# A two-block network on one core: the first block's mixers with all weight remainders on VectorE, and masked scores ahead of the short convolution

## The reference

```
h = rmsnorm(x, g_mix);  z = h @ w_in        # cut into a_b a_c a_h g_u g_v q k v q_idx k_idx w_idx d_a d_g
y_a = a_b * causal_dwconv3(a_c * a_h)
y_b = g_u * (tril(w_s) @ layernorm(g_v) + b_s)          # per chunk of 128 tokens and head
y_c = attention(rope(q), rope(k), v) over the 64 keys with the best index score
y_d = silu(layernorm(causal_dwconv31(d_a * sigmoid(d_g)) + b))
x = x + concat(y_a, y_b, y_c, y_d) @ w_out
x = x + (silu(rmsnorm(x) @ w_gate) * (rmsnorm(x) @ w_up)) @ w_down
```

## Time and profile before

| | us |
|---|---|
| median of 3 runs | 1291.46 (1290.04 to 1295.35) |
| the profiled execution | 1293.9, span 1292.1 |
| TensorE matmuls busy | 1145.1 (89%) |
| VectorE busy | 972.3 (75%) |
| ScalarE busy | 658.9 (51%) |
| GpSimd busy | 195.7 (15%) |

### The profile page before, as it was taken

How to read it: one execution, slowest core, us unless ns; L and a number is a source line. 1 busy time by engine, 2 the same in 40 slices (tenths; PEclk the granted TensorE clock), 3 DMA queues, 4 the chain that set the end, 5 groups by cost and what they waited for, 6 DMA issues and landing times.

```text
span 1292.1 us, 17395 instructions
## 1 busy us (share of the span) xinstructions
PE 1145.1 (89%) x6560; PEld 992.5 (77%) x6560; DVE 972.3 (75%) x1516; ACT 658.9 (51%) x935; POOL 195.7 (15%) x169
## 2 busy tenths in 40 slices
PE   3878779999997686799999899996499999999996
PEld 3757579999986485699999895674488888888885
DVE  5699669888546997588986544365888898889887
ACT  5323443333343233444443344534388888978885
POOL 4544100000034533000000100173300000000000
PEclk9879789999988796899999899997599999999998
DMA  9313136665742213467765511104157778787873
GB/s 381 134 65 129 67 130 230 242 246 225 278 181 82 104 45 151 186 270 319 306 262 220 206 66 66 65 1 179 82 227 294 301 285 315 276 318 275 320 274 139
DMA packets 23523, 256.52 MB, mean 199 GB/s; under 512 B 3120, under 2 KB 3248, under 8 KB 4912
## 3 DMA queue, kind: packets, MB, share of 16 engines
q1 hardware_dynamic: 23472, 255.86, 51.0%
HBM read 254.80 MB, written 1.05 MB: 198 GB/s over the span
## 4 chain that ended last, share of the span: by engine, by line
PE 75%; DVE 18%; issue 3%; ACT 2%; DMA 1%; POOL 1%; SPq 0%; DVEq 0%; POOLq 0%; ACTq 0%
PE bank L638 21%; PE bank L640 20%; PE bank L639 20%; DVE scratch L1676 5%; PE bank L629 3%; PE bank L1127 3%; PE bank L1110 3%; DVE w_l L1634 1%; DVE h_l L1640 1%; PE bank L898 1%; DMA m<-in_w_in 1%; DVE scratch L1775 1%; DVE w_l L2068 1%; DVE scratch L1730 1%; PE bank L973 1%
## 5 line engine op out<-in xcount | busy, mean ns | idle before, releaser
L2068 DVE TENSOR_TENSOR w_l<-m,w_h 128x1024 fp32r<-128x1024 f32 x196 | 239.2, 1254 | 19.8 <-ACT w_h L1499 19.5
L640 PE MATMUL bank<-h_h,fw_l 128*128 128x256 f32 x800 | 224.4, 281 | 0.0
L638 PE MATMUL bank<-h_h,fw_h 128*128 128x256 f32 x704 | 199.6, 284 | 8.3 <-issue 8.3
L1499 ACT ACTIVATE w_h<-m 128x1024 fp32r<-128x1024 f32 x200 | 198.0, 1050 | 14.0 <-DMA m<-in_experts 13.9
L639 PE MATMUL bank<-h_l,fw_h 128*128 128x256 f32 x704 | 197.8, 281 | 0.0
L1835 DVE TENSOR_TENSOR fw_l<-blocks_w,fw_h 128x1024 fp32r<-128x1024 f32 x132 | 156.3, 1220 | 2.9 <-ACT fw_h L1336 2.5
L640 PEld LDWEIGHTS bank<-h_h,fw_l 128*128 128x128 f32 x800 | 152.1, 190 | 0.0
L638 PEld LDWEIGHTS bank<-h_h,fw_h 128*128 128x128 f32 x704 | 133.5, 190 | 10.4 <-issue 8.7
L639 PEld LDWEIGHTS bank<-h_l,fw_h 128*128 128x128 f32 x704 | 134.0, 190 | 1.8
L1336 ACT ACTIVATE fw_h<-blocks_w 128x1024 fp32r<-128x1024 f32 x132 | 129.7, 1050 | 3.8 <-DMA blocks_w<-in_ffn 3.8
L1356 ACT ACTIVATE acts<-bank 128x256 f32<-128x256 f32 x44 | 16.9, 385 | 220.4 <-PE bank L640 220.4
(11 more groups left out here) (367 smaller groups left out, 2679.4 us busy)
## 6 DMA issues: line engine op xcount, KB each, us to landing
m<-in_experts SPq DMA_DIRECT2D x50, 2048.0 KB, 7.4
blocks_w<-in_ffn SPq DMA_DIRECT2D x22, 2048.0 KB, 7.6
m<-in_w_ada SPq DMA_DIRECT2D x24, 1024.0 KB, 8.4
m<-in_w_in SPq DMA_DIRECT2D x11, 2048.0 KB, 13.7
blocks_w<-in_ffn SPq DMA_DIRECT2D x22, 1024.0 KB, 4.9
m<-in_w_out SPq DMA_DIRECT2D x6, 2048.0 KB, 7.3
blocks_w<-in_w_in SPq DMA_DIRECT2D x2, 2048.0 KB, 21.3
m<-in_b_ada SPq DMA_DIRECT2D x2, 2048.0 KB, 7.7
```

The source lines that it names most:

```text
L638: pe.matmul(out_, xh, wh, start=first and i == 0, stop=False, skip_group_check=True)
L640: ins = pe.matmul(out_, xl, wh, start=False, stop=last and i == n - 1, skip_group_check=True)
L1499: act.activation(w_h[:, c % 3, at], m[:, c % 4, at], ACT.Copy).then_inc(hi_ready, 1)
L2068: dve.tensor_tensor(w_l[:, c % 4, at], m[:, c % 4, at], f32(w_h[:, c % 3, at]), ALU.subtract).then_inc(lo_ready, 1)
```

## The change

- All 30 remainders of a layer, and the rotation of q and k (`rotate_qk`), are on VectorE. GpSimd keeps norms, masks and the scaling of g_v.
- The rounded weights have other places: dadg in slot 3 of `m`, vqi in scratch, qk, ah and abac in `blocks_w`. So guv is loaded into slot 3 only when da and dg are done; abac and ah are loaded earlier; dg is computed before da, ah before ac and ab. `acc` of layer 0 is slot 1, so layer 1's qk is loaded behind the modulation sums.
- Layer 1's dadg and vqi are rounded and split during layer 0's FFN (blocks 7 to 9 and the last); its dadg is loaded after the first two pieces of `w_ada`.
- Of the 32 modulation sums 12 stay at the end of the FFN; 4 come before each of the two `tx1` transposes and 12 behind them. The sums are in bank 5 instead of 6.
- The four remainders of the first half of w_out are in rounds 4 to 7 of the top-k loop, those of the second half behind the normed convolution.
- On VectorE, after the loop: input of the short convolution, gated rows, masked scores, short convolution and its product with ab, remainders of y_b and y_a, then the statistics and norm of the long convolution. `cvT` is transposed behind the logits and `cnT` behind the first four parts of the output projection. ScalarE takes the exponentials ahead of y_a's rounding and of the silu.

The diff, cut to its core:

```diff
-IN_SUBS = 18
-DVE_STEPS, POOL_STEPS = 123, 14
+IN_SUBS = 30
+DADG, VQI, QK, AH, GUV, ABAC, OUT0, OUT1 = 0, 4, 8, 12, 14, 18, 22, 26
+DVE_STEPS, POOL_STEPS = 129, 8
...
-        vqi_h = fw_l[:, 1, 0:4096]
-        dadg_h = rounded_place("dadg_h", "scratch", riT_at, 4096)
+        vqi_h = rounded_place("vqi_h", "scratch", high_at, 4096)
+        qk_h, ah_h = fw_l[:, 1, 0:4096], fw_l[:, 1, 4096:6144]
...
-        acc = [m[:, 3, :], m[:, 2, :]]
+        acc = [m[:, 1, :], m[:, 2, :]]
...
-                sp.dma_start(m[:, 2, :], w_in("dadg")).then_inc(m_in[2], 16)
-                if l:
+                if l == 0:
+                    sp.dma_start(m[:, 2, :], w_in("dadg")).then_inc(m_in[2], 16)
+                else:
                     sp.wait_ge(ada_step, ADA_STEPS * l)
                 sp.dma_start(m[:, 0, :], w_in("vqi")).then_inc(m_in[0], 16)
-                sp.dma_start(m[:, 1, :], w_in("qk")).then_inc(m_in[1], 16)
+                if l == 0:
+                    sp.dma_start(m[:, 1, :], w_in("qk")).then_inc(m_in[1], 16)
                 sp.dma_start(lnrow.rearrange("p r n -> p (r n)"), a["gmlp_ln"][l].partition_broadcast(P)).then_inc(rows_ws_in, 16)
                 sp.dma_start(wsT.rearrange("p h n -> p (h n)"), a["w_s"][l]).then_inc(rows_ws_in, 16)
                 if l == 0:
                     sp.dma_start(prm2[:, :], a["prm2"]).then_inc(prm2_in, 16)
                 else:
+                    layer_results(l - 1).ready(sp, "y3")
+                sp.dma_start(blocks_w[:, 0, 4096:6144], w_in("ah")).then_inc(ah_in, 16)
+                if l:
                     layer_results(l - 1).ready(sp, "mod")
+                    sp.dma_start(m[:, 1, :], w_in("qk")).then_inc(m_in[1], 16)
+                sp.dma_start(blocks_w[:, 0, 0:4096], w_in("abac")).then_inc(ab_in, 16)
+                res.ready(sp, "da")
+                res.ready(sp, "dg")
                 sp.dma_start(m[:, 3, :], w_in("guv")).then_inc(m_in[3], 16)
-                src = w_in("abac")
-                sp.wait_ge(drained[3], l * LAY.count[3] + 1)
-                sp.dma_start(blocks_w[:, 0, 0:4096], src).then_inc(ab_in, 16)
-                sp.dma_start(blocks_w[:, 0, 4096:6144], w_in("ah")).then_inc(ab_in, 16)
                 for s, job in ((0, "vqi1"), (1, "qk1")):
                     src = a["w_out"][l, :, s * 4096:(s + 1) * 4096]
                     res.ready(sp, job)
                     sp.dma_start(m[:, s, :], src).then_inc(m_in[s], 16)
                 src = ffn_part(0, 0, GU)
-                res.ready(sp, "ah")
+                res.ready(sp, "ab")
...
+                if l == 0:
+                    sp.dma_start(m[:, 2, :], a["w_in"][1, :, IN_AT["dadg"]:IN_AT["dadg"] + 4096]).then_inc(m_in[2], 16)
...
+            def modulation_sums(l, which):
+
+                mod = layer_results(l)
+                if 0 in which:
+                    pe.wait_ge(ada_step, ADA_STEPS * (l + 1))
+                    mod.room(pe, "mod")
+                for o in which:
+                    n, k, row = (o // 16, o // 2 % KD, o % 2) if l == 0 else (o // KD, o % KD, 0)
+                    at = ((4 * row + 2 * n if l == 0 else 2 + 2 * n) + k // 4) * 512 + k % 4 * P
+                    col = (n * KD + k) * 2 + row
+                    ins = pe.matmul(bank[5][:, col:col + 1], acc[l][:, at:at + P], const[:, K_ONES:K_ONES + 1],
+                                    start=True, stop=True)
+                if len(which) and which[-1] == (31 if l == 0 else 15):
+                    mod.done(ins, "mod")
...
+                        if l and name == "tx1":
+                            modulation_sums(l - 1, range(12 + 4 * t, 16 + 4 * t))
...
+                if l:
+                    modulation_sums(l - 1, range(20, 32))
...
+                pe.wait_ge(in_lo, IN_SUBS * l + DADG + 4)
+                split_features("dg", w_l[:, 3, :], w_l[:, 2, :], T)
+                split_features("da", w_l[:, 3, :], w_l[:, 2, :], 0)
+                pe.wait_ge(in_lo, IN_SUBS * l + VQI + 4)
+                for t in range(NT):
+                    split_tokens("vqi", vqi_h[:, :], w_l[:, 0, :], t)
+                pe.wait_ge(in_lo, IN_SUBS * l + QK + 4)
+                for t in range(NT):
+                    split_tokens("qk", qk_h, w_l[:, 1, :], t)
...
-                pe.wait_ge(in_lo, 6 * l + 4)
+                pe.wait_ge(in_lo, IN_SUBS * l + GUV + 4)
                 for t in range(NT):
                     split_tokens("guv", w_l[:, 2, :], w_l[:, 3, :], t)
-                pe.wait_ge(ab_lo, 6 * l + 6)
-                split_features("ab", vqi_h, fw_l[:, 0, 0:4096], 0)
-                split_features("ac", vqi_h, fw_l[:, 0, 0:4096], 256)
-                split_features("ah", fw_l[:, 1, 4096:6144], fw_l[:, 0, 4096:6144], 0)
-
-                pe.wait_ge(conv_ready, l + 1)
-                res.room(pe, "cvT")
-                for t in range(NT):
-                    for g in range(2):
-                        ins = pe.transpose(to("cvT")[:, t * T + g * P:t * T + (g + 1) * P],
-                                           conv[:, g, t * P:(t + 1) * P], ident)
-                res.done(ins, "cvT")
+                split_features("ah", ah_h, fw_l[:, 0, 4096:6144], 0)
+                pe.wait_ge(in_lo, IN_SUBS * l + ABAC + 4)
+                split_features("ac", qk_h, fw_l[:, 0, 0:4096], 256)
+                split_features("ab", qk_h, fw_l[:, 0, 0:4096], 0)
...
-                pe.wait_ge(out_lo, 6 * l + 2)
-                pe.wait_ge(in_lo, 6 * l + 6)
+                pe.wait_ge(in_lo, IN_SUBS * l + OUT0 + 4)
                 pe.wait_ge(mix_ready, 4 * l + 2)
                 out_proj((0, 1, 2, 3), True, False)
+                res.arrived(pe, "cvT")
+                res.room(pe, "cnT")
+                for g in range(2):
+                    for t in range(NT):
+                        ins = pe.transpose(to("cnT")[:, g * T + t * P:g * T + (t + 1) * P],
+                                           conv_n[:, t, g * P:(g + 1) * P], ident)
+                res.done(ins, "cnT")
...
+                modulation_sums(l, range(12) if l == 0 else range(16))
...
+                if l == 0:
+                    act.wait_ge(m_in[2], 16)
+                    rounded_in(w_l[:, 3, :], m[:, 2, :], range(4))
                 for n in range(4):
                     t, b = n // 2, n % 2
                     part = (slice(None), slice(4 * b, 4 * b + 4), slice(t * P, (t + 1) * P))
                     res.arrived(act, f"tx1_{t}{b}")
                     act.activation(h1_h[part], hT[part], ACT.Copy).then_inc(h1_rounded, 1)
-                act.wait_ge(m_in[0], 32 * l + 16)
-                rounded_first(vqi_h, m[:, 0, :])
+                if l == 0:
+                    act.wait_ge(m_in[0], 16)
+                    rounded_in(vqi_h, m[:, 0, :], range(4))
+                act.wait_ge(m_in[1], 32 * l + 16)
+                rounded_in(qk_h, m[:, 1, :], range(4))
...
+                act.wait_ge(ah_in, 16 * l + 16)
+                rounded_in(ah_h, blocks_w[:, 0, 4096:6144], range(2))
...
+                vqi_copy(0)
+                act.wait_ge(m_in[3], 16 * l + 16)
+                rounded_in(w_l[:, 2, :], m[:, 3, :], (0, 1))
+                vqi_copy(1)
+                rounded_in(w_l[:, 2, :], m[:, 3, :], (2, 3))
                 qk_copy(0)
-                act.wait_ge(m_in[3], 16 * l + 16)
-                rounded_in(w_l[:, 2, :], m[:, 3, :], range(4))
                 qk_copy(1)
+                act.wait_ge(ab_in, 16 * l + 16)
+                rounded_in(qk_h, blocks_w[:, 0, 0:4096], (0, 1))
                 for t in range(NT):
                     res.ready(act, f"riT{t}")
                     copy(f"riT{t}", riT[:, :, t * P:(t + 1) * P], to(f"riT{t}")[:, 0:3 * P].rearrange("p (c q) -> p c q", c=3))
+                rounded_in(qk_h, blocks_w[:, 0, 0:4096], (2, 3))
...
-                rounded_mix(0, "ab")
                 res.ready(act, "ybT")
                 copy("ybT", yT[:, 2:4, :], to("ybT")[:, :].rearrange("p (k t) -> p k t", k=2))
                 rounded_mix(1, "ybT")
-                res.ready(act, "cnT")
-                for g in range(2):
-                    ins = act.activation(yT[:, 6 + g, :], to("cnT")[:, g * T:(g + 1) * T], ACT.Silu,
-                                         scale=prm[:, C_LNG + g:C_LNG + g + 1], bias=prm[:, C_LNB + g:C_LNB + g + 1])
-                res.moved(ins, "cnT")
-                rounded_mix(3, "cnT")
...
+                rounded_mix(0, "ab")
+                res.ready(act, "cnT")
+                for g in range(2):
+                    ins = act.activation(yT[:, 6 + g, :], to("cnT")[:, g * T:(g + 1) * T], ACT.Silu,
+                                         scale=prm[:, C_LNG + g:C_LNG + g + 1], bias=prm[:, C_LNB + g:C_LNB + g + 1])
+                res.moved(ins, "cnT")
+                rounded_mix(3, "cnT")
...
+                    if l == 0 and b == 7:
+                        act.wait_ge(m_in[2], 32)
```

(73 more changed lines are left out.)

151 lines of the change are left out of this document (48 added, 103 removed), and 4 rows, old and new, of the table b.

## The result

The changed kernel takes 1242.99 us (median of 4 runs, 1241.33 to 1245.03) against 1291.16 for the kernel before on the same chip (4 runs, 1290.04 to 1295.35). The ratio is 0.9622, 95% interval 0.9595 to 0.9649: 48 us faster. 1238 was forecast, range 1226 to 1256.

The account below looks back on a forecast made before the run. VectorE's program order was taken to bound the mixers, TensorE layer 0's FFN. Layers give -26.6 and -27.0, together -53.6: profiled 1293.9 becomes 1240.3; that execution stood 2.4 above the median, so 1238 us, range 1226 to 1256.

Parts of the forecast that it names:

- Rival 2: VectorE's slowness isn't GpSimd's doing and taps keep their price: 27 us slower, 1318 us; chance 0.03.
- (a): Start of the taps: first taps come earlier, -7.9 us in layer 0 and -8.6 in layer 1.
- (b): First taps to first index score: 32.3 us at clean prices, -16.1 and -16.0 in the two layers.
- Rival 1: The weight loads (guv, layer 1's qk) become the wait: +14.7 us, 1253 us; chance 0.14.
- (c): First index score to output projection: 45.4 us against 49.7, ScalarE the late one; -4.3 and -4.1.
- (d): Behind the projection's start: silu and a rounding come ahead of three copies the attention product needs; +1.7 us a layer.
- (e): Layer 0's FFN takes 8 roundings, 8 remainders and one 2 MB load beside full TensorE: 0.

Follow-up runs that it names:

- experiment 3: Kernel before, own order, with only its 18 GpSimd remainders a layer moved to VectorE; q/k rotations stay on GpSimd; 1246.67 us.
- experiment 1: Changed kernel plus 22 unread two-input GpSimd operations (128x512) a layer, VectorE's program untouched; 1281.58 us.
- experiment 5: Changed kernel with all 32 modulation sums of layer 0 in one row at the end of its FFN; 1240.84 us.
- experiment 8: Changed kernel plus masked scores behind short convolution, split projection with c's statistics ahead, v normalised one round earlier, layer 0's sums at its FFN end; 1225.49 us.
- experiment 10: Changed kernel with masked scores behind short convolution, split projection with c's statistics ahead, v normalised one round earlier; sums left between the transposes; 1223.77 us.
- Experiment 4: Changed kernel with VectorE's masked scores again behind the short convolution, and ScalarE's mixer roundings ahead of the exponentials; 1228.74 us.
- Experiment 6: Changed kernel with VectorE's normalisation of v in top-k round 5 instead of 6; 1238.09 us.
- experiment 2: Changed kernel plus 22 unread GpSimd copies (128x512, one input) a layer; 1253.52 us.
- Experiment 9: Changed kernel plus 21 unread 128x512 products in TensorE's 7.57 us wait ahead of the output projection; 1237.3 us.

## Why the prediction was right, point by point

The profiled spans fell by 48.9 us (1292.1 to 1243.2), against 53.6 forecast.

**The mechanism.** GpSimd's help cost VectorE more than the work. Shown: the work alone, moved, gives 45 us (experiment 3), GpSimd work alone, put back, takes 39 (experiment 1). Rival 2 is false. GpSimd's busy time fell from 195.7 to 91.7 us, as said; the taps read 0.475 us in the median and 0.485 at most.

**(a), layer 0,** forecast -7.9: first taps 44.28 to 37.38, -6.9. In the ten experiments that leave the start as it is they come at 36.1 to 37.0, so -7.9 lies among these and the profiled run is a late one. **Layer 1,** forecast -8.6, measured from its first addition to x: 39.9 to 33.5, -6.4. This is the one term that was clearly mis-sized. I took kwi at its full-clock 3.76; it took 7.07, and the first da/dg products also ran at half speed. TensorE had no gap in the whole stretch (busy 33.55 of 33.55), so that start hangs on its clock (0.75), not on the load and ScalarE as I wrote. The sums' place was suspected; experiments 5, 8 and 10 (33.3, 36.0 and 35.1 us, the first two in one row, the third as in the kernel after) don't pin it down. Interleaving isn't what made the clock fall: it fell in the kernel before too, where the sums are one row, with TensorE busy without a gap. Granted clock (third number from the end) from the sums on, before and then after:

```profile
371.00:372.00 1.00, 1.00 (x11) 1.00 (x10) 0.88 (x1) 1.00 (x2) 0.95 (x2) 0.94 0.00 0
...
373.00:380.00 7.00, 7.00 (x34) 7.00 (x34) 1.90 (x3) 1.02 (x2) 3.25 (x2) 0.50 0.18 37
...
383.00:386.00 3.00, 3.00 (x30) 3.00 (x28) 3.00 (x3) 3.00 (x4) 1.98 (x1) 1.00 0.98 421
```
```profile
349.00:350.00 1.00, 1.00 (x10) 1.00 (x10) 1.00 (x2) 0.49 (x1) 0.00 (x0) 0.82 0.00 0
...
352.00:364.00 12.00, 12.00 (x57) 12.00 (x58) 2.85 (x7) 0.82 (x3) 0.00 (x0) 0.50 0.57 217
...
366.60:376.00 9.40, 9.40 (x82) 9.40 (x81) 5.27 (x6) 5.23 (x10) 0.00 (x0) 0.99 0.13 54
```

Before, it was back by the time kwi began (382.60), and my 3.76 was read there; after, it came back only at 366.6, behind kwi and the first da/dg products. What brings it back sooner or later stays open.

**(b)** forecast -16.1 and -16.0: -16.3 and -16.2. The stage laid out instruction by instruction at clean prices was right to 0.2 us (32.3 forecast, 32.11 and 32.10). The q/k rotation estimated at 2.1 us took 2.0. The loads came in time: VectorE waits 0.85 us in the whole stretch, for ScalarE's copy ahead of the first rotation. Rival 1 is false.

**(c)** forecast -4.3 and -4.1: -4.0 and -4.4. The late one is ScalarE's chain, as written: copy 107.65, rounding, table, exponentials to 113.8, rounding, and the remainder at 114.38 behind 2.25 us of VectorE's idle time. What I didn't see is what follows from it. I had 41 for VectorE alone in the same sum and took ScalarE's 45.4 as the stage's price rather than as the price of the order. Experiment 4 shows that the order of the two engines costs 5.9 and 5.3 us of this stage and about 1 more behind it in each layer. Moving a step ahead of the last one is worth nothing if a third engine then has it in front of the same last one.

The Trainium skill, page "SBUF — State Buffer", section "SBUF: two separate sides", was weighed here: by its lock the last out-projection remainder would be held by up to 0.83 us a layer. The collision came, but the held one was GpSimd: its product took 1.79 us instead of 0.82 beside the remainder, the next mixer product was late, and VectorE waited 0.98 us. Experiment 6 takes the wait away. The page's condition of two SBUF inputs is on VectorE's side, where the taps have them (it names a two-port mode of VectorE as the other); on GpSimd's side it asks only that the operation read SBUF, and copies with one input held the taps one for one (experiment 2). I read the earlier trace rows wrongly as its support: GpSimd's 0.83 us product had ended at 122.66 when the match-replace began at 122.83. It ran beside the next one and still took 0.28 us, so the case stands on this row:

```profile
122.74 0.73 POOL L2343 TENSOR_TENSOR acts<-acts,scratch 128x256 f32<-128x256 f32 x1
```

**(d)** forecast +1.7: +2.5 and +2.2. The order cost what was said; the rest is the clock. The projection's products at the lower level were 9 before and 13 after, 4 x 0.19 = 0.8 us. The granted clock was at the lower level when the projection began in both: before, it had been since 130 us at least; after, it was 1.00 from 107.6 to 110 and fell within TensorE's wait of 7.57 us. Experiment 9 shows the clock's whole share.

**(e)** forecast 0: nothing in the FFN proper of layer 0, but the way from the last addition to the first silu grew by 1.1 and 0.8 us. What follows the FFN of layer 1 is 1.7 us shorter, which the sum didn't have.

## What to carry to other kernels

Where VectorE is full and GpSimd busy beside it, price VectorE's operations from a stretch where GpSimd is silent before giving GpSimd any work: here 18 remainders a layer taken back gained 45 of 1291 us, and the same forecast came out right to 0.2 us for a stage because it used clean prices only. When a step is moved ahead to feed another engine, write down that engine's queue and ask who waits behind it: the exponentials beside the projection were free, in front of it they cost 5 to 6 us a layer. Once VectorE's waits are gone, look at the granted clock of what follows: a start 1.4 us earlier was lost to a clock that was low already ahead of it, and a few unread products in TensorE's waits brought it back.
